# A ninth 2 MB weight place, from a smaller scratch for dynamic transfers and shared small buffers; first loads and odd weights dealt out anew

## The reference

```python
def expert_choice_moe(x, w_router, w_gate_up, w_down):
    cap = CAPACITY_FACTOR * S // N_EXPERTS            # 32 tokens for each expert
    aff = softmax(x @ w_router, axis=-1)
    gates, idx = lax.top_k(swapaxes(aff, 1, 2), cap)
    xs = x[bi, idx]
    g, u = split(einsum('becd,edf->becf', xs, w_gate_up), 2, axis=-1)
    out = einsum('becf,efd->becd', silu(g) * u, w_down) * gates[..., None]
    return zeros_like(x).at[bi, idx].add(out)
```

## Time and profile before

| what | value |
|---|---|
| median of three runs | 1467.5 us |
| the profiled execution's span, first to last instruction | 1466.6 us |
| PE busy / DVE / ACT / POOL | 1123.2 / 469.5 / 323.6 / 74.8 us |
| read from HBM | 498.92 MB |
| moved over the whole span | 341 GB/s |
| transfers' share of the chain that ended last | 46% |

### The profile page before, as it was taken

The page is one execution under the profiler, slowest core; times in us unless marked ns, Lnnn a source line. Parts: engine busy times, 40 slices in busy tenths (PEclk is TensorE's granted clock), DMA queues, the critical chain, the costliest instruction groups (busy, mean ns, idle before and its releaser), DMA issues.

```text
span 1466.6 us, 19642 instructions
## 1 busy us (share of the span) xinstructions
PE 1123.2 (77%) x8637; PEld 637.1 (43%) x8637; DVE 469.5 (32%) x948; ACT 323.6 (22%) x618; POOL 74.8 (5%) x100
## 2 busy tenths in 40 slices
PE   8999856679485656899985565655656699989998
PEld 6756312245131211698641111211211289744897
DVE  4537202100220100587640100100010067564874
ACT  4422110001320000366210000000000046533550
POOL 3000100000000000042020000000000000000100
PEclk9999977799788877999998878888787799999999
DMA  9967999999999999938999999999999964133830
GB/s 301 351 223 287 401 425 423 426 417 421 427 425 424 427 426 424 373 115 322 422 380 425 425 426 428 427 425 425 429 426 426 420 245 151 62 126 131 283 122 29
DMA packets 92988, 501.29 MB, mean 342 GB/s; under 512 B 7534, under 2 KB 16196, under 8 KB 61160
## 3 DMA queue, kind: packets, MB, share of 16 engines
q1 hardware_dynamic: 87728, 492.78, 83.2%
q10 hardware_dynamic: 3112, 5.96, 1.2%
q0 software_dynamic: 2064, 1.30, 0.3%
HBM read 498.92 MB, written 1.10 MB: 341 GB/s over the span
## 4 chain that ended last, share of the span: by engine, by line
DMA 46%; PE 36%; DVE 8%; ACT 5%; SPq 2%; issue 1%; ACTq 0%; POOL 0%; DVEq 0%
DMA weight_ring<-in_moe_w_gate_up 27%; DMA weight_ring<-in_moe_w_down 16%; PE bank L1401 6%; PE bank L341 5%; PE bank L632 3%; PE bank L1431 3%; PE bank L342 3%; PE bank L344 3%; PE bank L343 3%; DMA weight_ring<-in_even_w_in 2%; SPq L527 2%; PE bank L1849 1%; DVE weight_ring_rounded L382 1%; PE bank L941 1%; DMA weight_ring<-in_attn_w_qkv 1%
## 5 line engine op out<-in xcount | busy, mean ns | idle before, releaser
L1401 PE MATMUL bank<-weight_ring,expert_tokens 128*32 128x512 f32 x1904 | 286.5, 737 | 175.0 <-DMA weight_ring<-in_moe_w_gate_up 170.1
L1401 PEld LDWEIGHTS bank<-weight_ring,expert_tokens 128*32 128x32 f32 x1904 | 61.6, 123 | 373.5 <-DMA weight_ring<-in_moe_w_gate_up 209.4
L1431 PE MATMUL bank<-weight_ring,actT 128*32 128x256 f32 x1824 | 148.3, 484 | 60.7 <-DMA weight_ring<-in_moe_w_down 52.3
L1639 DVE TENSOR_TENSOR act<-silu,bank 128x256 f32<-128x256 f32 x32 | 13.4, 420 | 419.6 <-ACT silu L1755 419.6
L1431 PEld LDWEIGHTS bank<-weight_ring,actT 128*32 128x32 f32 x1824 | 67.9, 134 | 131.1 <-DMA weight_ring<-in_moe_w_down 55.6
L1755 ACT ACTIVATE silu<-bank 128x256 f32<-128x256 f32 x32 | 12.3, 384 | 463.7 <-PE bank L1401 463.7
L1653 DVE COPY expert_outs<-bank 32x256 f32<-32x256 f32 x60 | 25.1, 418 | 231.1 <-PE bank L1431 230.1
L382 DVE TENSOR_TENSOR weight_ring_rounded<-weight_ring,weight_ring_rounded 128x1024 fp32r<-128x1024 f32 (+1 forms) x76 | 89.2, 1234 | 18.0 <-ACT weight_ring_rounded L366 17.8
L366 ACT CAST weight_ring_rounded<-weight_ring 128x1024 fp32r<-128x1024 f32 (+1 forms) x72 | 70.0, 1043 | 38.5 <-DMA weight_ring<-in_attn_w_qkv 12.8
L1772 ACT COPY expert_outs<-bank 32x256 f32<-32x256 f32 x60 | 21.9, 364 | 209.3 <-PE bank L1431 208.6
L496 POOL TENSOR_TENSOR norm_rstd<-norm_var,minus_half 128x1 f32<-128x1 f32 x12 | 12.1, 1008 | 910.7 <-DVE norm_var L1688 658.1
(11 more groups left out here) (526 smaller groups left out, 1865.2 us busy)
## 6 DMA issues: line engine op xcount, KB each, us to landing
weight_ring<-in_moe_w_gate_up SPq DMA_DIRECT2D x119, 2048.0 KB, 32.4
weight_ring<-in_moe_w_down SPq DMA_DIRECT2D x57, 2048.0 KB, 31.7
weight_ring<-in_ada_w SPq DMA_DIRECT2D x9, 2048.0 KB, 10.3
weight_spare<-in_moe_w_gate_up SPq DMA_DIRECT2D x9, 2048.0 KB, 35.6
weight_ring<-in_even_w_in SPq DMA_DIRECT2D x5, 2048.0 KB, 9.4
weight_ring<-in_odd_w_in SPq DMA_DIRECT2D x5, 2048.0 KB, 12.8
weight_ring<-in_lru_w_in SPq DMA_DIRECT2D x4, 2048.0 KB, 17.4
weight_spare<-in_ada_w SPq DMA_DIRECT2D x3, 2048.0 KB, 15.0
```

The lines of the kernel that those rows point to most:

```text
L1401: last = pe.matmul(up[CAP * j:CAP * (j + 1), :], B.xs[:, t, e * CAP:(e + 1) * CAP], w[:, t % 2, :, j, :], start=(t == 0), stop=(t == T - 1))
L1431: last = pe.matmul(K[3][CAP * q:CAP * (q + 1), 0:QC], B.actT[i][:, s, j * CAP:(j + 1) * CAP], w[:, jj, s, q, :], start=(j == 0 and s == 0) ...
```

## The change

There are now eight places in the ring (0 to 7) and the spare one (8). Layer 0 goes round eight places and layer 1 round nine. The memory comes from a descriptor scratch of 2048 in place of 16384 bytes a partition, and from buffers that now share memory: `ada_rows` lies in a part of `xT`, `gate_rows` in the router's weights, `two` in `gelu`, small context buffers in `left` and `places`. Because of the first two of these, the bias loads on POOL's queue wait until the router's products of their layer have ended (event "router_parts"), and those of layer 0 are issued at the head of `modulation_store_pool`.

The main part of the diff:

```diff
-SLOTS = 7
+SLOTS = 8
 SPARE = SLOTS
-TAIL_SLOT = 3
+TAIL_SLOT, TAIL_END = 3, 7
@@ units()
-    turn = [1, 2, 3, 4, 5, 6, 0]
+    turn = list(range(SLOTS))
-        state["slots"], state["at"] = ring if layer else ring[:SLOTS], 0
+        state["slots"], state["at"] = ring if layer else [slot for slot in ring if slot != SPARE], 0
...
-    state["slots"], state["at"] = [0, 1, 2], 0
+    state["slots"], state["at"] = [0, 1, 2, 7], 0
...
-    put(f"ada1{GATE_BLOCKS[0]}", 2)
-    state["slots"], state["at"] = [3, 4, 5, 6, 0, 1, 2], 0
-    for slot in range(TAIL_SLOT, SLOTS):
+    put("odd_f", 0)
+    put("odd_f_hi", 1)
+    for slot in range(TAIL_SLOT, TAIL_END):
         occupant[slot] = "latents"
...
+    put(f"ada1{GATE_BLOCKS[0]}", 3)
+    put("odd_sv", 5)
+    put("odd_sv_hi", 6)
+    put(f"ada1{GATE_BLOCKS[1]}", 4)
@@ attention_pool
-        self.modulation_bias_pool(0)
@@ modulation_bias_pool
+        g.wait_ge(*sig.after("router_parts", f"moe{layer}", 1))
@@ modulation_store_pool
+        self.modulation_bias_pool(layer)
         g.wait_ge(*sig.after("ada_rows", layer))
@@ gate_bias_pool
+        g.wait_ge(*sig.after("router_parts", "moe1", 1))
@@ recurrent_pool
-        g.wait_ge(*sig.after("grown", 1))
-        self.modulation_bias_pool(1)
@@ buffers
-    B.spare_at = M.size - UNIT - 504
+    B.spare_at = M.size - UNIT - 112
-    B.ada_rows = M.place("ada_rows", M.at, [NA, P])
+    B.ada_rows = M.place("ada_rows", xT_at + 1024, [NA, P])
@@ kernel
-    nc = bacc.Bacc("TRN2", target_bir_lowering=False, num_devices=1)
+    nc = bacc.Bacc("TRN2", target_bir_lowering=False, num_devices=1, dynamic_dma_scratch_size=2048)
```

More of the change, by code:

```diff
@@ L289, in units @@
             for name, i in (("lru2", 0), ("lru2_hi", 1), ("lru3", 2), ("lru3_hi", 3), ("rgate", 4), ("igate", 5), ("lru0", 6),
-                            ("lru0_hi", 0), ("decay_room", 1), ("lru1", 2), ("lru1_hi", 3), ("lru_out0", 4), ("lru_out1", 5)):
+                            ("lru0_hi", 0), ("decay_room", 1), ("lru1", 2), ("lru1_hi", 3), ("lru_out0", 7), ("lru_out1", 4)):
                 put(name, first[i])
             turn = first
-    state["slots"], state["at"] = [0, 1, 2], 0
+    state["slots"], state["at"] = [0, 1, 2, 7], 0
     for i, (name, _) in enumerate(EVEN_W):
@@ L300, in units @@
     put("even_out1")
-    put(f"ada1{GATE_BLOCKS[0]}", 2)
-    state["slots"], state["at"] = [3, 4, 5, 6, 0, 1, 2], 0
-    for slot in range(TAIL_SLOT, SLOTS):
+    put("odd_f", 0)
+    put("odd_f_hi", 1)
+    for slot in range(TAIL_SLOT, TAIL_END):
         occupant[slot] = "latents"
[L305 to L313, removed]
+    put(f"ada1{GATE_BLOCKS[0]}", 3)
+    put("odd_sv", 5)
+    put("odd_sv_hi", 6)
+    put(f"ada1{GATE_BLOCKS[1]}", 4)
+    for name, slot in (("odd_su", 2), ("odd_su_hi", 7), ("odd_fg", 3), ("odd_fg_hi", 4), ("odd_sg", 0), ("odd_sg_hi", 1),
+                       ("odd_out0", 5), ("odd_out1", 6), ("odd_out0_hi", 2), ("odd_out1_hi", 7)):
+        put(name, slot)
     return order
@@ L3133, in buffers @@
     B.minus_half, B.sink, B.rope = M.take("minus_half", 8), M.take("sink", NQ), M.take("rope", H, 2, ROT // 2)
-    B.slot_no, B.router = M.take("slot_numbers", CAP), M.take("router", DEPTH, T, NE)
+    B.slot_no, B.gate_rows = M.take("slot_numbers", CAP), M.place("gate_rows", M.at + CAP, [2, P])
+    B.router = M.take("router", DEPTH, T, NE)
     B.columns, B.parameter_rows = M.take("parameter_columns", 96), M.take("parameter_rows", P)
@@ L3196, in buffers @@
     B.ctx_hT = M.take("context_features", T, S)
+    assert M.at <= B.spare_at + UNIT
+    M.at = left_at
     B.ctx_stats, B.ctx_mv = M.take("ctx_stats", H, 12), M.take("ctx_mv", H, 2)
@@ L3199, in buffers @@
     B.ctx_junk, B.ctx_ss, B.ctx_r = M.take("ctx_junk", KVR), M.take("ctx_ss", H), M.take("ctx_r", H)
+    assert M.at <= left_at + 2 * S
     M.at = mark
-    B.ctx_z, B.ctx_t, B.ctx_sums = M.take("ctx_z", 4, S), M.take("ctx_t", 4, S), M.take("ctx_sums", S + 1)
+    B.ctx_z, B.ctx_t, B.ctx_sums = M.take("ctx_z", 4, S), M.take("ctx_t", 4, S), M.place("ctx_sums", left_at, [S + 1])
     B.ctx_wk, B.ctx_wkT = B.ctx_t[:, 2, :], B.ctx_t[:, 0:2, :]
@@ L3208, in buffers @@
     B.ex, B.sq, B.acc, B.decay, B.growth = (M.take(n, 16) for n in ("lam_ex", "lam_sq", "lam_acc", "decay", "growth"))
-    B.stack, B.gate_rows = M.take("stacked_identity", 2 * NE), M.take("gate_rows", 2, P)
+    B.stack = M.take("stacked_identity", 2 * NE)
+    assert M.at <= M.size
     M.at = room
@@ L3215, in buffers @@
     B.I = [M.take("i0", T, S), M.place("i1", padded_at, [T, S])]
-    B.two = [M.take(f"two{i}", 2, S) for i in range(2)]
+    B.two = [M.place(f"two{i}", gelu_at + 2 * S * i, [2, S]) for i in range(2)]
     assert M.at <= B.spare_at
```

13 lines of the change are left out of this document (8 added, 5 removed).

## The result

| | kernel before | kernel changed |
|---|---|---|
| median | 1467.59 us (1467.0 to 1468.32, 4 runs) | 1459.6 us (1457.95 to 1459.94, 4 runs) |
| ratio to before | | 0.9944, 95% interval 0.9932 to 0.9956 |
| profiled execution, its span | 1466.6 us | 1459.53 us, 1457.9 us |

The change makes the kernel 8.0 us faster. The forecast was 9.9 us: the time lies 2.0 us above its 1457.6 us, inside the range of 1455.0 to 1463.0, and 0.6 us outside the forecast's own range of 1456.3 to 1459.0.

A forecast was written before the change was run, and what follows sets the result against it. The expert stages were taken to be bound by DMA transfers that never rest, so only earlier stream beginnings help. Gains of 4.95 + 4.92 = 9.87 us bring the median of 1467.5 to 1457.6 us; range 1455.0 to 1463.0.

The forecast's parts named there:

- Layer 0, 4.95 us: Start and layer 0: the unbroken stream begins at 146.94 with one unit fewer behind it, 4.95 us off the layer's end.
- Cover in attention: Attention: the extra unit ahead of `ada03` makes it land at 77 us; PE wants it at 89.86, 12 us of slack.
- Recurrent block and layer 1, 4.92 us: After `lru1`, `lru_out0` fills a hole in the transfers; layer 1's stream has one unit fewer behind it, 4.92 us.
- What lies outside the span, 0.9 us: Part of the 1467.5 us median outside the profiled span, added to the predicted span of 1456.7: 0.9 us.
- Steady rounds: Expert plateaus with eight and nine places: 0 gained; issue to landing rises to about 36 and at most 41 us.
- scratch: Smaller descriptor scratch: bias loads still about 0.5 us each of POOL's time, so 0.
- tail: Even and odd stages: between 0 and 1.07 and between 0 and 0.3 us gained, each taken as 0.
- bias loads: POOL's loads behind the router land by 140 to 144 us, at least 13 us before DVE reads them: 0.
- One lead only: Rival: one of the two stream beginnings gets no earlier, another SP wait eating the unit; 1462.6 us, chance 0.07.
- PE the real bound: Rival: PE at low clock bounds the experts in the plateaus, so earlier units only lie longer; 1467.5 us, chance 0.04.
- More than the lead: Rival: a deeper queue closes dents where the streams begin, and tail waits are gained, 5.2 us more; 1452.4 us, chance 0.07.
- Slower by POOL: Rival: small scratch makes bias loads wait for one another, 12.9 us late in each layer; 1483.4 us, chance 0.06.

The follow-up runs named there:

- bias loads made twice: Changed kernel with POOL waiting for each bias load's landing and each load made twice: 1499.25 us, 39.7 more than the changed kernel.
- the first run with layer 1's place alone: Changed kernel with the ninth place withheld from layer 0, whose first units are dealt as in the kernel before: 1468.29 us, ratio 1.0003.
- the old dealing: Changed kernel with even-stage weights in three places and odd-stage ones in a round of seven, as in the kernel before: 1458.8 us, ratio 0.9939.
- the one-by-one run: Changed kernel in which POOL waits, after each of a layer's eight bias loads, for its landing: 1459.1 us, ratio 0.9941.

## Why the prediction was right, and where its sizes were off

*What bounds the kernel* holds: DMA share is 1.01 in both plateaus of every run but the one with the bias loads made twice, in which the transfers stood still, and the time follows the rate (11.0 us with 428 for 424 GB/s) and the beginnings, not the depth.

*Layer 0, 4.95 us.* It was 4.4 in the profiled run, where PE's clock had dropped in attention, and 5.0 to 5.2 in the traces of the same dealing, with the ring at its old remainder, in which it stayed up. So the size was right. What didn't hold in the profiled run is the prediction's premise that these waits "are ended by PE's work, which doesn't change": a lead is worth only what is left after the waits ahead of it have slipped. The clock fell in two of the nine traces with the new first loads and in none of the five with the old ones; whether those loads bring it about is not settled.

*Cover in attention.* `ada03` landed at 80.5 us, for 77 worked out and 89.86 needed. PE wasn't held up.

*Recurrent block and layer 1, 4.92 us.* The lead rose by 5.0 from the end of layer 0 (4.4) to `down1_2_1` (9.4), and 4.2 were left at the layer's end. This is the term that was mis-sized: the prediction priced every unit alike at 4.92 us and the moved address of the spare at nothing. It was a fast place before and became an ordinary one, and in the stretch from 770 to 1145 us seven gate/up fills of the spare had been 0.05 us shorter and three down fills 0.11: 0.7 of the 0.8 us that drained away there. That the lead reached the end of the kernel was also in part luck: no step of the prediction looks at the place of the even stage's first unit, and the first run with layer 1's place alone shows that this place by itself can cost the whole lead.

*What lies outside the span, 0.9 us.* In the executions with a span on record it is 1.25 to 1.73 us. The 0.9 set the median of three runs beside a profiled span that was 0.3 to 0.6 us longer than the typical one (1466.0 to 1466.3). With 1.6 the same two leads give 1458.3: 0.7 of the 2.0 us by which the forecast was too low.

*Steady rounds, scratch, tail, bias loads: 0 each.* All four shown, by a run of their own or by the loads' 4.05 us and DVE without a wait. In the odd stage `ada15` comes 1.0 us later than forecast, PE waits 1.32 us for it instead of 0.31:

```profile
1353.61 1.93 PE L938 MATMUL bank<-weight_ring,condition_columns 128*2 128x128 f32 x64 [1.32 <-DMA weight_ring<-in_ada_w]
```

The end shows nothing of it that the runs could tell: with the old dealing the time was 1458.8.

*The rivals.* One lead only: refuted, though the first run with layer 1's place alone shows how near it lay. PE the real bound: refuted, since faster fills alone gave the kernel before 9.4 us. More than the lead: not by closing dents. The window from 147 to 166 moved 379 GB/s for 391, and 395 to 398 in the traces where the clock stayed up; the second dent moved 9 us earlier and is no shallower (731 to 759: 374 GB/s, for 392 from 740 to 768). Slower by POOL: didn't come, and its price was wrong. It let 12.9 us of a late bias go into each layer in full; 14.6 and 18.9 us cost nothing, because units already issued went on landing. The deciding point was not 3.4 us a load: it lay beyond the 5.3 us of the one-by-one run, and by the run with the loads made twice the stock covers some 24 and 29 us. The prediction had the stock in its own latencies (about 36 and 41 us) and didn't use it.

## What to carry to other kernels

Where transfers bind without a break, a further buffer is worth one unit at each place where the stream begins, if the waits hand it down and no unit at the exit of the stage sits in a place that comes free late; depth beyond that only buys tolerance of stalls. The time from issue to landing bounds that tolerance from above: here it was 36 and 41 us, and stalls of some 24 and 29 us were covered. Before paying 2 MB for a buffer, look at the start address of those that exist: moving seven of them by 128 bytes a partition was worth 9.4 us in the kernel before, more than the ninth place. And where one of several equal buffers is faster in the trace, its address is the first thing to ask about.

## What the hardware showed that I had not expected

Destinations that start at a multiple of 256 bytes in the partition fill about 1% faster in pieces of 16 KB (4.85 for 4.90 us) and 1.4 to 2% faster in pieces of 8 KB (4.90 for 4.97 in layer 0, 4.87 for 4.97 in layer 1), with the DMA engines' share at 1.01 in either case, so that the busy share doesn't betray it. The granted clock can fall behind a wait of 1.53 us in one execution and stay up behind one of 1.54 us in another.
